# A hybrid decoder trunk: the last tile before each output projection signals its channel tiles as it reads them, and new high and low parts are written while it still runs

## The chip, the cores and the metric

The kernel runs on one core of a Trainium2 chip. The metric is the device time of one execution in microseconds (us), as the median of several runs.

## The reference, cut to what matters

One step of two layers for 512 prompt tokens and 64 sampled tokens (8 sequences of 8), 576 tokens in all, 2048 channels, in float32:

```python
# layer 0: attention (A) and gated DeltaNet (B) share one input projection
h = rms_norm(x, norm_gain[0])
qa, ka, va, za, qkv_b, a_b, b_b, z_b = split_even(h @ w_in_even[0])
o_a = attention(qa, ka, va) * silu(za)            # channels 0..1023 of the output's input
o_b = rms_norm(delta_rule(...)) * silu(z_b)       # channels 1024..2047
x = x + concatenate([o_a, o_b]) @ w_out_even[0]   # first output projection
# layer 1: Conformer convolution module
h = rms_norm(x, norm_gain[1])
val, gate, z = split(h @ w_in_odd[0], 3)
c = layer_norm(conv31(val * sigmoid(gate)) + conv_b)
y = silu(c) * silu(z)
x = x + y @ w_out_odd[0]                          # second output projection
out = rms_norm(x, final_norm_gain)                # and the new caches and states
```

## The kernel before

Activations lie channel-major: 16 channel tiles of 128 channels by 576 tokens, each kept three times. `full[:, k, :]` holds tile k in float32, `act_hi[:, k, :]` a rounded high part, `act_lo[:, k, :]` the rest (`full - act_hi`). Weights are split in the same way into `w_hi` and `w_lo`, in two slots. A product of one weight tile (128 output channels) is 96 matmuls of 128x288: for each of the 16 channel tiles and each half of the tokens `w_hi*act_hi`, `w_hi*act_lo` and `w_lo*act_hi`. They add up in one of two PSUM slots, `acc`. A **tile** below is such a set of 96 matmuls. All tiles stand in one list; `N_OUT0` and `N_OUT1` are the first tiles of the two output projections, `N_OUT0 - 1` (the last gate tile of the attention branch, `za`) and `N_OUT1 - 1` (the last `z` tile of the convolution module) are the tiles just ahead of them.

The order on each engine is written out by hand, and engines wait for one another on counting semaphores. TensorE runs tile after tile: `proj` (line 577) does a pair of channel tiles, e = 0 to 7, and counts `w_used` after e = 3 and e = 7; `first_tile` (line 604) does the first tile of an output projection in another order, high parts first and low parts `LOW_LAG` steps behind (12 in the first projection, 2 in the second), with a wait for each channel tile's part (`ahi_done`, `alo_even`, `alo_odd`). ScalarE copies weights to `w_hi` (`split_hi`) and channel tiles to `act_hi` (`act_split`; both are line 1088), computes the gate's tanh (`z_tanh`, line 1375, and `z_tanh_`, line 1481), and `affine` (lines 1487 and 1492). VectorE makes `w_lo` (`split_lo`) and every other tile of `act_lo` (`act_lo_even`; both line 1540), GpSimd the rest of `act_lo` (`act_lo_odd`, line 2268). SyncE issues the loads of weights (`w_raw`) and of the residual (`res`).

`act_hi` and `act_lo` exist once. The old parts are read by the last tile of the stage, so the new ones of the output projection are written after it:

```python
if turn == 1:
    act.wait_ge(w_used, 2 * n0)      # all of tile N_OUT0 - 1 has been read
    act_split(turn, 0, 8)            # channel tiles 8..15 (DeltaNet)
    act.wait_ge(gated, 1)            # sampled columns of tiles 0..7 are gated
act_split(turn, 8)                   # channel tiles 0..7 (attention)
```

In the first projection, `za_product(i)` on VectorE gates channel tile i of the attention branch with the product of gate tile i: it scales the prompt's columns of `full[:, i]`, and puts the gate of the sampled columns aside in `zs_samp`. Behind the last one, two instructions gate the sampled columns of tiles 0 to 7 together; the first of them lets SyncE load the residual (`res_free`), the second lets ScalarE go on (`gated`). Before them VectorE waits for stores of caches (`out_small`, `vnew_stored`).

In the second projection, step t of a loop on ScalarE and VectorE runs while TensorE does z tile t. `LN_Y` says at which t a channel tile's normalised value goes through `affine` and the two products that give y (`y_done`); tiles 13 and 14 stand at t = 15, tile 15 at t = 16, which is the time of tile `N_OUT1`, behind `act_split(3, 0, 6)`, the last `z_tanh_` and `act_split(3, 6, 8)`.

## Time and profile before

| what | value |
|---|---|
| median of 3 runs | 2012.45 us (2009.88 to 2012.73) |
| the profiled execution | 2012.49 us, of which the span is 2010.7 us |
| TensorE (PE) busy | 1966.4 us, 98% of the span |
| VectorE (DVE), ScalarE (ACT), GpSimd (POOL) busy | 1234.1, 733.6, 669.4 us |
| mean granted TensorE clock | 0.995 |

The span is the time from the first to the last instruction in the trace. In a timeline row the first number is the start in us from the beginning of the span, the second how long the row's instructions took together, `xN` how many there are, and the bracket how long the engine stood idle before and whose work ended that. PEld is the weight load of TensorE, SPq and ACTq the DMA issues of those engines.

### The profile page before, as it was taken

The numbers are of one execution on the slowest core, as the hardware profiler recorded it, in microseconds if no ns is written. First come the engines' busy times: TensorE is split into PE (matmuls) and PEld (weight loads), VectorE is DVE, ScalarE is ACT, GpSimd is POOL, SyncE is SP. The second block draws the span as 40 slices with busy tenths as digits, with TensorE's granted clock in tenths as the row PEclk, the third lists the DMA queues.
The fourth block names the chain that finished last, engine by engine and source line by source line (L and its number), as shares of the span: only waits on it lengthen the run. The fifth ranks groups of instructions, "written<-read, shape, count | busy, mean of one in ns | idle before, by whom it ended". The sixth has DMA issues, their size and how long they took to land.

```text
span 2010.7 us, 37345 instructions
## 1 busy us (share of the span) xinstructions
PE 1966.4 (98%) x15596; PEld 1905.2 (95%) x15596; DVE 1234.1 (61%) x2458; ACT 733.6 (36%) x1268; POOL 669.4 (33%) x659
## 2 busy tenths in 40 slices
PE   6999999999999999999999999999999999999997
PEld 4999999999999989898999999999999999999997
DVE  6566666656663436663433389999999954463334
ACT  5422222222222124552312255555555533342220
POOL 5123212321231121001211158888888850021110
PEclk9999999999999999999999999999999999999999
DMA  6211212212122334121444333333333222223333
GB/s 194 74 64 56 64 65 64 65 56 75 54 73 84 116 117 161 53 64 58 128 131 132 108 107 92 90 91 95 95 95 94 87 77 73 85 81 120 105 103 117
DMA packets 79721, 184.14 MB, mean 92 GB/s; under 512 B 26776, under 2 KB 35928, under 8 KB 79304
## 3 DMA queue, kind: packets, MB, share of 16 engines
q1 hardware_dynamic: 72304, 166.22, 27.0%
q0 software_dynamic: 3504, 9.63, 1.4%
q10 hardware_dynamic: 3744, 5.90, 0.8%
q8 instruction: 123, 2.02, 0.4%
q14 instruction: 46, 0.38, 0.1%
HBM read 162.66 MB, written 19.06 MB: 90 GB/s over the span
## 4 chain that ended last, share of the span: by engine, by line
PE 49%; DVE 2%; issue 0%; ACT 0%; DMA 0%; POOLq 0%; POOL 0%; DVEq 0%
PE acc L577 46%; PE acc L649 2%; DVE full L1543 1%; DVE act_lo L1540 1%; PE acc L604 1%; DVE w_lo L1540 0%; PE gp L619 0%; PE acc L677 0%; PE acc L666 0%; DMA w_raw<-wt 0%; PE gp L628 0%; ACT act_hi L1088 0%; DVE full L1540 0%; ACT w_hi L1088 0%; DVE arena L1581 0%
## 5 line engine op out<-in xcount | busy, mean ns | idle before, releaser
L577 PE MATMUL acc<-act_hi,w_hi 128*128 128x288 f32 x3904 | 860.8, 302 | 0.4 <-DVE w_lo L1540 0.3
L577 PE MATMUL acc<-act_hi,w_lo 128*128 128x288 f32 x3904 | 836.5, 296 | 0.0
L577 PE MATMUL acc<-act_lo,w_hi 128*128 128x288 f32 x3904 | 835.8, 296 | 0.0
L577 PEld LDWEIGHTS acc<-act_hi,w_hi 128*128 128x128 f32 x3904 | 624.9, 189 | 14.8 <-issue 9.5
L577 PEld LDWEIGHTS acc<-act_hi,w_lo 128*128 128x128 f32 x3904 | 628.8, 189 | 0.0
L577 PEld LDWEIGHTS acc<-act_lo,w_hi 128*128 128x128 f32 x3904 | 627.8, 189 | 0.0
L2268 POOL TENSOR_TENSOR arena<-arena 128x512 f32<-128x512 f32 (+2 forms) x281 | 387.0, 1377 | 347.6 <-ACT arena L1384 283.9
L1088 ACT ACTIVATE w_hi<-w_raw 128x1024 fp32r<-128x1024 f32 x264 | 277.1, 1054 | 420.6 <-PE acc L577 308.7
L1540 DVE TENSOR_TENSOR w_lo<-w_raw,w_hi 128x1024 fp32r<-128x1024 f32 x264 | 380.5, 1461 | 41.3 <-ACT w_hi L1088 40.5
L1543 DVE SCALAR_TENSOR_TENSOR gp<-arena,par,gp 128x64 f32<-128x64 f32 (+1 forms) x688 | 248.2, 445 | 0.0
L1088 ACT ACTIVATE arena<-arena,par 128x512 f32<-128x512 f32 x240 | 165.1, 720 | 96.4 <-POOL arena L2268 88.6
L1540 DVE TENSOR_TENSOR full<-acc,arena 128x576 f32<-128x576 f32 (+1 forms) x36 | 24.8, 689 | 232.9 <-PE acc L577 215.0
L2268 POOL TENSOR_TENSOR arena<-arena,cst 128x24 f32<-128x24 f32 (+2 forms) x82 | 31.3, 393 | 266.4 <-DVE arena L1543 109.8
L2268 POOL TENSOR_TENSOR act_lo<-full,act_hi 128x288 fp32r<-128x288 f32 (+1 forms) x48 | 57.7, 1223 | 157.8 <-ACT act_hi L1088 157.7
L2268 POOL TENSOR_TENSOR small<-small 128x4 f32<-128x4 f32 (+5 forms) x87 | 47.6, 552 | 141.2 <-DVE small L1547 76.2
L2268 POOL TENSOR_TENSOR full<-full,cst 128x512 f32<-128x512 f32 x40 | 60.5, 1521 | 66.3 <-PE gp L773 49.9
L1088 ACT ACTIVATE arena<-gp 128x512 f32<-128x512 f32 (+5 forms) x54 | 27.8, 540 | 133.7 <-PE gp L879 49.7
L1543 DVE SCALAR_TENSOR_TENSOR arena<-arena,small 128x512 f32<-128x512 f32 (+2 forms) x145 | 68.5, 515 | 0.3
L1543 DVE SCALAR_TENSOR_TENSOR arena<-arena,acc 128x576 f32<-128x576 f32 x24 | 18.0, 750 | 80.2 <-ACT arena L1481 74.0
L1088 ACT ACTIVATE act_hi<-full 128x288 fp32r<-128x288 f32 (+1 forms) x96 | 45.3, 516 | 33.4 <-DVE full L1543 29.1
L1088 ACT ACTIVATE full<-gp 128x256 f32<-128x256 f32 (+1 forms) x40 | 15.2, 379 | 113.7 <-PE gp L773 107.3
L1540 DVE TENSOR_TENSOR full<-full,gp 128x576 f32<-128x576 f32 (+2 forms) x72 | 32.8, 489 | 32.0 <-PE gp L788 26.2
(263 smaller groups left out, 1792.2 us busy)
## 6 DMA issues: line engine op xcount, KB each, us to landing
w_raw<-wt SPq DMA_DIRECT2D x264, 512.0 KB, 4.0
full<-x SPq DMA_DIRECT2D x16, 288.0 KB, 6.7
arena<-x SPq DMA_DIRECT2D x16, 288.0 KB, 3.6
arena<-x_scratch SPq DMA_DIRECT2D x16, 288.0 KB, 2.8
x_scratch<-full ACTq DMA_DIRECT2D x14, 288.0 KB, 4.0
out_y<-full SPq DMA_DIRECT2D x24, 144.0 KB, 1.9
arena<-state_in SPq DMA_DIRECT2D x6, 512.0 KB, 4.1
out_sdn<-arena POOLq DMA_DIRECT2D x6, 512.0 KB, 3.1
```

The lines of the kernel that those rows point to most:

```text
L577: ins = pe.matmul(acc[:, s, i, 0:HALF], w[:, s, wk], a[:, k, i * HALF:(i + 1) * HALF], start=(k == 0 and j == 0), stop=(k == KT - 1 and j ...
L604: ins = pe.matmul(acc[:, s, i, 0:HALF], w[:, s, wk], a[:, k, i * HALF:(i + 1) * HALF], start=(not low and pos == 0 and j == 0), stop=(low ...
L649: ins = pe.matmul(acc[:, s, a, 0:HALF], w[:, s, wk], x_[:, k, token_half(a)], start=(k == 0 and j == 0), stop=(k == KT - 1 and j == 2))
L1088: return act.activation(out, in_, ACT.Copy, scale=scale)
L1540: return dve.tensor_tensor(out, a, b, op)
L1543: return dve.scalar_tensor_tensor(out=out, in0=a, scalar=scalar, in1=b, op0=op0, op1=op1)
L2268: return pool.tensor_tensor(out, a, b, op)
```

## The change

For the last tile before each output projection, TensorE counts a new semaphore, `act_used`, after each pair of channel tiles that has no `w_used` of its own. `act_split` waits for the pair that it overwrites instead of for the whole tile.

In the first projection the order of the channel tiles becomes 0 to 5, 8 to 15, 6, 7. ScalarE begins twelve of them ahead of the last gate tanh, and the other four behind it. Sampled columns of tiles 0 to 6 are gated during tile `N_OUT0 - 1`, behind the gating of tile 6, and those of tile 7 by themselves behind the gating of tile 7. The waits for the stores move from VectorE to SyncE, in front of its loads of the residual.

In the second projection, channel tile 15 moves from t = 16 to t = 15, and its first product with it ahead of the last `z_gate`. `act_split(3, 0, 6)` goes to t = 15, six more follow ahead of the last `z_tanh_`, three behind it, and tile 15 comes last. `act_lo_even` goes along.

```diff
@@ -175,7 +175,7 @@
 
 LN_SQ = {3: range(0, 6), 4: range(6, 12), 5: range(12, 16)}
 LN_Y = {7: (0, 1), 8: (2, 3), 9: (4, 5), 10: (6, 7), 11: (8, 9)} | {k + 2: (k,) for k in range(10, 13)}
-LN_Y |= {15: (13, 14), 16: (15,)}
+LN_Y |= {15: (13, 14)}
 SAD = counts(["bias0", "bias1", "bias2", "max", "max2", "neg", "sub", "den", "inv", "prob", "turned_new",
               "out0", "out1"])
 SAA = counts(["exp", "turned", "v_new0", "v_new1"])
@@ -207,7 +207,7 @@
 def split_order(turn):
 
 
-    return [(k + 8) % KT for k in range(KT)] if turn == 1 else list(range(KT))
+    return [*range(6), *range(8, KT), 6, 7] if turn == 1 else list(range(KT))
 
 
 def blk(c):
@@ -359,6 +359,7 @@
         sdn_stored = [sem(f"sdn_stored{i}") for i in range(4)]
         ys_done = sem("ys_done")
         gated, halved = sem("gated"), sem("halved")
+        act_used, half_y = sem("act_used"), sem("last_y_without_gate")
         samp_pe, samp_dve = sem("samp_pe"), sem("samp_dve")
         samp_act, samp_pool = sem("samp_act"), sem("samp_pool")
 
@@ -370,7 +371,7 @@
         sa_pe, sa_dve, sa_act = sem("sa_pe"), sem("sa_dve"), sem("sa_act")
 
         res_in = [sem("res_in0"), sem("res_in1")]
-        res_free, x1_stored = sem("res_free"), sem("x1_stored")
+        x1_stored = sem("x1_stored")
 
         u_free, uprev_in = [sem("u_free0"), sem("u_free1")], [sem("uprev_in0"), sem("uprev_in1")]
         cf_stored = sem("cf_stored")
@@ -528,7 +529,9 @@
                 weights(n0)
                 weights(n0 + 1)
                 if n0 == N_OUT0:
-                    sp.wait_ge(res_free, 1)
+                    sp.wait_ge(gated, 1)
+                    sp.wait_ge(out_small, 16 * n_small)
+                    sp.wait_ge(vnew_stored, 32)
                 else:
                     sp.wait_ge(acc_free[0], N_VG // 2 + 1 + KT)
                     sp.wait_ge(x1_stored, 16 * X1_STORES)
@@ -563,7 +566,7 @@
 
         @block.tensor
         def _(pe):
-            def proj(m, s, e):
+            def proj(m, s, e, frees_act=False):
 
                 half = e // 4
                 if e % 4 == 0:
@@ -578,10 +581,12 @@
                                             start=(k == 0 and j == 0), stop=(k == KT - 1 and j == 2))
                 if e % 4 == 3:
                     ins.then_inc(w_used, 1)
-
-            def tile_of(m, s):
+                elif frees_act:
+                    ins.then_inc(act_used, 1)
+
+            def tile_of(m, s, frees_act=False):
                 for e in range(8):
-                    proj(m, s, e)
+                    proj(m, s, e, frees_act)
 
             def first_tile(n, turn):
 
@@ -1015,7 +1020,7 @@
                 n = N_Q + t
                 for e in range(8):
                     slot = 8 * t + e
-                    proj(n // 2, n % 2, e)
+                    proj(n // 2, n % 2, e, frees_act=(t == 15))
                     if slot == 0:
                         head_step(H - 1, 1, "o_chan")
                     if slot < ATT0 - 1:
@@ -1076,7 +1081,7 @@
             for i in range((N_Z1 + 7) // 2, N_OUT1 // 2):
                 tile_of(i, 0)
                 tile_of(i, 1)
-            tile_of(N_OUT1 // 2, 0)
+            tile_of(N_OUT1 // 2, 0, frees_act=True)
             out_section(N_OUT1, 3)
             half_sums(3, 1)
             spread_roots(NORM_END + 1, HALF_CHUNKS[1])
@@ -1106,8 +1111,15 @@
             def act_split(turn, first=0, last=KT):
 
                 for k in split_order(turn)[first:last]:
+                    e, half = k // 2, k // 8
                     if turn == 3:
                         act.wait_ge(y_done, k + 1)
+                    else:
+                        act.wait_ge(gated, 2 if k == 7 else 1)
+                    if e % 4 == 3:
+                        act.wait_ge(w_used, 2 * (N_OUT0 if turn == 1 else N_OUT1) - 1 + half)
+                    else:
+                        act.wait_ge(act_used, 6 * (turn // 2) + e + 1 - half)
                     copy(act_hi[:, k, :], full[:, k, :]).then_inc(ahi_done, 1)
 
 
@@ -1370,6 +1382,7 @@
                                     .then_inc(sa_act, 1)
 
             n = N_OUT0 - 1
+            act_split(1, 0, 12)
             tile_done(n // 2, n % 2)
             act.wait_ge(acc_free[1 - n % 2], (n - 1) // 2 + 1)
             act.activation(halves(za_t), acc_of(n % 2), ACT.Tanh, scale=0.5).then_inc(z_tanh, 1)
@@ -1386,11 +1399,7 @@
                         act.dma_start(x1_dram[j], full[:, j, :]).then_inc(x1_stored, 16)
 
 
-                if turn == 1:
-                    act.wait_ge(w_used, 2 * n0)
-                    act_split(turn, 0, 8)
-                    act.wait_ge(gated, 1)
-                act_split(turn, 8)
+                act_split(turn, 12 if turn == 1 else KT - 1)
                 split_hi((n0 + 1) // 2, (n0 + 1) % 2, 0)
                 split_hi((n0 + 1) // 2, (n0 + 1) % 2, 1)
                 for j in (1, 2):
@@ -1509,13 +1518,15 @@
                     if k >= 2:
                         act.wait_ge(c_summed, KT + k - 1)
                     act.activation(sqb[k % 2], full[:, k, :], ACT.Square).then_inc(ln_sq, 1)
-                if t == KT:
-                    act.wait_ge(w_used, 2 * N_OUT1)
+                if t == KT - 1:
                     act_split(3, 0, 6)
-                    z_tanh_(t - 1)
-                    act_split(3, 6, 8)
                 for k in LN_Y.get(t, ()):
                     affine(k)
+                if t == KT - 1:
+                    affine(KT - 1)
+            act_split(3, 6, 12)
+            z_tanh_(KT - 1)
+            act_split(3, 12, KT - 1)
             out_section(N_OUT1, 3)
             post_half(N_OUT1, 3, KT - 2, 1)
 
@@ -2020,6 +2031,13 @@
                                               gp[:, 2, 0:256].rearrange("p (j a c) -> p j a c", j=4, a=2)[:, :, a_, :])
                     ins.then_inc(sa_dve, 1)
 
+            def gate_samples(first, last):
+
+                for a_ in range(2):
+                    dst = full[:, first:last, a_ * HALF + HP:(a_ + 1) * HALF]
+                    ins = stt(dst, zs_samp[:, first:last, a_, :], 0.5, dst, MUL, MUL)
+                return ins
+
             own = lambda n_: dve.wait_ge(sa_dve, SAD[n_])
             for t in range(16):
                 n = N_Q + t
@@ -2039,19 +2057,18 @@
                         samp_att(SATT_DVE[slot - SATT0])
                     if e == 4 and t > 8:
                         za_product(t - 9)
+                        if t == 15:
+                            own("out1")
+                            for n_ in (N_ZA + 5, N_ZA + 6):
+                                dve.wait_ge(acc_free[n_ % 2], n_ // 2 + 1)
+                            gate_samples(0, 7).then_inc(gated, 1)
                     next_split(n // 2, n % 2, e)
-            act_lo_even(1, 8)
+
+            for k in split_order(1)[0:11:2]:
+                act_lo_even(1, k)
             za_product(7)
-
-            own("out1")
-            for n in (N_OUT0 - 2, N_OUT0 - 1):
-                dve.wait_ge(acc_free[n % 2], n // 2 + 1)
-            dve.wait_ge(out_small, 16 * n_small)
-            dve.wait_ge(vnew_stored, 32)
-            for a_ in range(2):
-                dst = full[:, 0:8, a_ * HALF + HP:(a_ + 1) * HALF]
-                stt(dst, zs_samp[:, :, a_, :], 0.5, dst, MUL, MUL).then_inc((res_free, gated)[a_], 1)
-
+            dve.wait_ge(acc_free[(N_ZA + 7) % 2], (N_ZA + 7) // 2 + 1)
+            gate_samples(7, 8).then_inc(gated, 1)
 
             def out_section(n0, turn):
                 def add_residual(m, s, j, jp, rnd):
@@ -2060,7 +2077,7 @@
                     dve.wait_ge(res_in[jp], 16 * rnd + (16 if turn == 1 else 16 + 8 * KT))
                     tt(halves(full[:, j, :]), acc_of(s), halves(res[jp]), ADD).then_inc(acc_free[s], 1)
 
-                for k in split_order(turn)[2 if turn == 1 else 8::2]:
+                for k in split_order(turn)[12 if turn == 1 else 10::2]:
                     act_lo_even(turn, k)
                 for half in range(2):
                     split_lo((n0 + 1) // 2, (n0 + 1) % 2, half)
@@ -2215,8 +2232,12 @@
             for t in range(1, KT + 1):
                 n = N_Z1 + t
                 if t == KT:
-                    for k in (0, 2, 4):
-                        act_lo_even(3, k)
+                    act_lo_even(3, 2)
+                    act_lo_even(3, 4)
+                    dve.wait_ge(ln_tanh, KT)
+                    stt(full[:, KT - 1, :], sqb[(KT - 1) % 2], 1.0, full[:, KT - 1, :], ADD, MUL).then_inc(half_y, 1)
+                    act_lo_even(3, 6)
+                    act_lo_even(3, 8)
                 if t > 1:
                     z_gate(t)
                 if 1 < t < KT:
@@ -2235,8 +2256,14 @@
                     dve.wait_ge(root_out, NORM_LN + 1)
                 for k in LN_Y.get(t, ()):
                     tt(halves(full[:, k, :]), halves(full[:, k, :]), rstd_ps, MUL).then_inc(ln_scaled, 1)
+                if t == KT - 1:
+                    tt(halves(full[:, KT - 1, :]), halves(full[:, KT - 1, :]), rstd_ps, MUL).then_inc(ln_scaled, 1)
+                    act_lo_even(3, 0)
                 if t == KT:
-                    act_lo_even(3, 6)
+                    k = KT - 1
+                    dve.wait_ge(half_y, 1)
+                    dve.wait_ge(acc_free[(N_Z1 + k) % 2], (N_Z1 + k) // 2 + 1)
+                    stt(full[:, k, :], full[:, k, :], 0.5, zring[k % ZRING], MUL, MUL).then_inc(y_done, 1)
                 for k in LN_Y.get(t, ()):
                     dve.wait_ge(ln_tanh, k + 1)
                     order(stt(full[:, k, :], sqb[k % 2], 1.0, full[:, k, :], ADD, MUL))
```

## Rows read from the trace of the kernel before

**Rows 1.** The page's first part: busy time, share of the span and instructions.
```profile
PE 1966.4 (98%) x15596; PEld 1905.2 (95%) x15596; DVE 1234.1 (61%) x2458; ACT 733.6 (36%) x1268; POOL 669.4 (33%) x659
```

**Rows 2.** Waits of PE over the span: us in total, times, longest.
```profile
PE acc L604 <- ACT act_hi L1088: 7.0, 4, 3.0
```

**Rows 3.** Stretches: length, busy us (count) of PE, PEld, DVE, ACT, POOL, granted clock, DMA share, GB/s.
```profile
933.40:946.30 12.90, 12.90 (x145) 12.58 (x144) 3.08 (x6) 0.00 (x0) 0.00 (x0) 1.00 0.26 81
946.30:965.80 19.50, 15.07 (x99) 14.64 (x98) 17.76 (x15) 11.83 (x19) 13.82 (x8) 0.91 0.10 31
965.80:978.60 12.80, 12.80 (x99) 12.80 (x98) 4.05 (x4) 3.75 (x4) 1.15 (x1) 1.00 0.65 211
...
1783.60:1802.58 18.98, 15.48 (x99) 14.45 (x97) 16.66 (x14) 13.28 (x21) 14.72 (x8) 0.91 0.00 1
```

**Rows 4.** Timeline of PE around the first projection's first tile.
```profile
946.03 0.42 PE L577 MATMUL acc<-act_hi,w_lo 128*128 128x288 f32 x2
947.86 0.50 PE L604 MATMUL acc<-act_hi,w_hi 128*128 128x288 f32 x2 [1.40 <-ACT act_hi L1088]
...
952.15 0.43 PE L604 MATMUL acc<-act_hi,w_lo 128*128 128x288 f32 x2
955.61 0.53 PE L604 MATMUL acc<-act_hi,w_hi 128*128 128x288 f32 x2 [3.03 <-ACT act_hi L1088]
...
956.95 0.68 PE L604 MATMUL acc<-act_hi,w_hi 128*128 128x288 f32 x2
...
959.83 0.54 PE L604 MATMUL acc<-act_lo,w_hi 128*128 128x288 f32 x2
...
965.80 0.43 PE L577 MATMUL acc<-act_hi,w_hi 128*128 128x288 f32 x2
```

**Rows 5.** Timelines of ACT and DVE there.
```profile
946.49 0.65 ACT L1375 ACTIVATE arena<-acc 128x576 f32<-128x576 f32 x1 [13.23 <-PE acc L577]
947.04 4.69 ACT L1088 ACTIVATE act_hi<-full 128x576 fp32r<-128x576 f32 x8
...
938.60 0.19 DVE L1987 COPY arena<-arena 128x64 f32<-128x64 f32 x1
938.70 1.22 DVE L1540 TENSOR_TENSOR w_lo<-w_raw,w_hi 128x1024 fp32r<-128x1024 f32 x1
...
951.88 2.96 DVE L1543 SCALAR_TENSOR_TENSOR full<-arena,full 128x256 f32<-128x256 f32 x2 [0.19 <-issue]
```

**Rows 6.** Timeline of PE around the second projection's first tile.
```profile
1783.34 0.43 PE L577 MATMUL acc<-act_hi,w_lo 128*128 128x288 f32 x2
1784.63 0.51 PE L604 MATMUL acc<-act_hi,w_hi 128*128 128x288 f32 x2 [0.86 <-ACT act_hi L1088]
...
1792.67 0.66 PE L604 MATMUL acc<-act_hi,w_hi 128*128 128x288 f32 x2 [1.69 <-ACT act_hi L1088]
...
1802.58 0.53 PE L577 MATMUL acc<-act_hi,w_hi 128*128 128x288 f32 x2 [0.35 <-DVE w_lo L1540]
```

**Rows 7.** Timelines of ACT, DVE and POOL there.
```profile
1772.03 0.63 ACT L1481 ACTIVATE arena<-acc 128x576 f32<-128x576 f32 x1
...
1775.64 1.41 DVE L1540 TENSOR_TENSOR full<-full,gp 128x576 f32<-128x576 f32 x2
1778.04 0.76 DVE L1543 SCALAR_TENSOR_TENSOR full<-arena,full 128x576 f32<-128x576 f32 x1 [0.99 <-ACT arena L1492]
...
1780.31 0.76 DVE L1543 SCALAR_TENSOR_TENSOR full<-full,arena 128x576 f32<-128x576 f32 x1
1784.52 0.76 DVE L1540 TENSOR_TENSOR act_lo<-full,act_hi 128x576 fp32r<-128x576 f32 x1 [3.45 <-ACT act_hi L1088]
...
1793.69 7.70 DVE L1540 TENSOR_TENSOR act_lo<-full,act_hi 128x576 fp32r<-128x576 f32 x4
1801.31 2.35 DVE L1540 TENSOR_TENSOR w_lo<-w_raw,w_hi 128x1024 fp32r<-128x1024 f32 x2
...
1793.27 7.50 POOL L2268 TENSOR_TENSOR act_lo<-full,act_hi 128x576 fp32r<-128x576 f32 x4 [0.91 <-ACT act_hi L1088]
```

## The prediction, made before the changed kernel was run

> **What bounds the kernel now.** I read the page's busy times first [rows 1]: TensorE is busy for 98% of the span, so a change can only win what TensorE still loses. Its list of waits comes next [rows 2]: of the waits that a software change can touch, the two `first_tile` runs (line 604) lose 7.0 us to high parts. A wait list misses slow matmuls, so I then measured both stretches from the last matmul pair of the old tile to the first of the next normal one [rows 3]. An undisturbed tile is 96 matmuls in 12.80 us, 0.133 us each, so a pair of them is due every 0.267 us. The two first tiles hold the same 96 matmuls but take 19.50 and 18.98 us: 6.70 and 6.18 us too much, 12.88 us together. That is the whole prize, 0.64% of the time.
>
> Where the 6.70 us lie in the first projection: the old tile's last pair starts at 946.03, the next would be due at 946.30 and starts at 947.86 (1.56 us) [rows 4], because ScalarE begins its high parts only at 947.04, after the tile's end and a tanh [rows 5]. After the first 8 channel tiles the pair due at 952.42 starts at 955.61 (3.19 us): the attention half waits for the gating of the sampled columns, two VectorE instructions at 951.88 that take 2.96 us. Then the matmuls run at 0.68 us a pair instead of 0.43, and the stretch has a granted clock of 0.91 where the next has 1.00: part of it ran at 1.2 GHz instead of 2.4. Six pairs from 956.95 to 959.83 take 2.88 us instead of 1.60, so 1.3 us. The remaining 0.65 us are a few more slow pairs, high parts that come every 0.57 us (8 take 4.69 us) while four matmuls eat one in 0.533 us, and small restarts. The second projection is alike [rows 6]: 1.03 us at the start (due 1783.60, starts 1784.63), 1.69 us of idling before 1792.67, about 1.7 us by a granted clock of 0.91 (0.09 x 18.98), and the other 1.8 us mostly late low parts and the next `w_lo`, for which PE waits at 1802.58.
>
> **The change, first projection.** The gating of tiles 0 to 6 now follows `za_product(6)`, whose last instruction ends at 938.79 [rows 5]. It is two instructions of 128x224. The nearest row, two of 128x256, took 2.96 us while GpSimd worked; GpSimd and ScalarE do nothing from 933.4 to 946.3 [rows 3], and the 128x64 copy there took 0.19 us. I take 0.4 us each, within 0.2 and 1.5: `gated` at 939.6 (939.2 to 941.8). The `w_lo` behind it moves by 0.8 us to 940.8; it is due at 946.3.
>
> ScalarE, idle before 946.49 for 13.23 us [rows 5], starts high parts at 939.7, one every 0.574 us: six by 943.2. Tiles 8 to 13 need `act_used` from e = 4, 5, 6. From the last e pairs back from 946.30 at 1.6 us each, e = 4, 5, 6 end at 941.5, 943.1, 944.7, so none of the six waits; the twelfth is done at 946.7. TensorE starts its first at 946.3 and needs one every 0.53 us, being seven to eleven ahead: the starting gap, the slow feed and the middle gap are gone, and with them the reason for the lower clock. The tanh moves from 946.49 to 946.7, behind the twelve.
>
> VectorE and GpSimd make the low parts from 940.8. Four pairs of them took 7.7 us where both worked [rows 7], 1.90 us a pair, though one alone on VectorE takes 0.76. So one blocks the other: 0.7 us for VectorE's, 1.2 for GpSimd's. Six on VectorE end at 940.8 + 0.7 + 5 x 1.9 = 951.0. Behind them stand, in VectorE's queue, `za_product(7)` (0.75, 0.7 and 0.2 us and up to 1.5 us of blocking: 954.2) and the gating of tile 7 (two of 128x32, taken at 0.2 us each because GpSimd has nothing left until tile 7's high part exists; up to 1.5 each): 954.6. Tile 7's high part is then ready at 955.3. TensorE wants it at its sixteenth step, 946.3 + 12 x 0.533 + 3 x 0.8 = 955.1. So about 0.2 us are lost, 2.8 at the upper bound. Then two low parts and the next `w_lo` follow: 958.4, due 959.1. First projection: 6.70 - 0.25 = **6.4 us won**.
>
> **Second projection.** ScalarE does six high parts in z tile 15 behind the tanh that ends at 1772.66 [rows 7]. It waits for e = 0, 1, 2 (1772.4, 1774.0 and 1775.6, counted back from 1783.60) and is done at 1777.0, before VectorE has scaled tile 13 for `affine`. VectorE's chain sets the end, so I follow it. Before, it finished y of tile 14 at 1781.07. Now GpSimd's first low part comes between the two `w_lo` (1.2 us), a third scaling by `rstd` is added (0.7), and the low part of tile 0 with its blocking (1.1); the 0.99 us of idleness ahead of 1778.04 absorbs as much. So 1781.07 + 1.2 + 0.7 + 1.1 - 1.0 = 1783.1. Then five instructions (low parts 2, 4, 6, 8 and the first product of tile 15) share with four of GpSimd's: 5 x 0.7 + 4 x 1.2 = 8.3, to 1791.4. `z_gate` and the last product of tile 15: 1.5, to 1792.9. Low parts 10, 12 and 14 and GpSimd's last: 3 x 0.7 + 1.2 = 3.3, to 1796.2. First `w_lo`: 1.2, to **1797.4**. TensorE alone would start the next tile at 1783.6 + 12.8 = 1796.4; low part 10 is 0.2 to 0.4 us late for it, the high part of tile 15 (1793.6) in time for 1795.1. Before, that tile started at 1802.58: **5.2 us won**; 6.2 if VectorE kept up, about 3.0 if each of its 11 instructions in that stretch took 0.2 us more.
>
> At this place the rows show 1.90 us for a low part on each of the two engines, against 0.76 us for one alone. The Trainium skill, SBUF — State Buffer, section Who interferes with whom, says that a VectorE instruction with two SBUF inputs and a GpSimd one that reads SBUF take a shared port exclusively, whoever comes first; that speaks against spreading low parts over a stage in which VectorE has work of its own. The trace agrees. Costed at 0.76 us each, VectorE would be done before TensorE and the second projection would win 6.2 us; by the rule, as by the row, 5.2.
>
> **What costs nothing.** The twelve new counts ride on matmuls. SyncE's new waits stand ahead of its residual loads and behind those all later weight loads; `gated` comes at 939.6, the stores' count was no wait on VectorE before (0.19 us idle before 951.88 [rows 5]), and the next weights cannot be asked for before a `w_lo` near 957. If a store were late the residual would still have until 959. Everything behind the first projection hangs on TensorE's progress and moves with it.
>
> **Sum.** 6.4 + 5.2 = 11.6 us. The profiled execution took 2012.49 us, 0.04 from the median: 2012.45 - 11.6 = **2000.9 us**.
>
> **The rivals.**
> (a) *A gap remains in one of the first tiles.* VectorE's queue with GpSimd's blocking is tight at 955.1 and 1793. If tile 7's gating is blocked (2.8 us) or low parts come 0.2 us later each (2.0 us), and a lower clock follows once more (1.3 to 1.7 us), some 4 us are lost: 2005. For it: the 2.96 us of the gating before. Against: GpSimd has no work at that moment. The Trainium skill, TensorE: Matmul & The Clock Gate, section HAM oscillation, says that idle gaps bring the slow clock back. The rows show it after the 3.19 us gap.
> (b) *One section gives nothing*, say since y of tile 15 now holds back the other tiles: 2012.45 - 6.4 = 2006.
> (c) *Given back later*, by a chain that does not start from TensorE: 2012. Against: no other engine is busy for more than 61% [rows 1].
> (d) *Slower.* All twelve high parts, and the tanh behind them in ScalarE's queue, now wait for one VectorE count. With `gated` at G the tile would end at about G + 0.7 + 12.8 + 0.4; that is 965.80 at G = 951.9, where the gating was before, and 4 us slower from 955.9 on: 2016 or more. It needs the gating 16 us later than reckoned, behind a `za_product(6)` that the trace shows done at 938.8.
> (e) *The change does not do what it says*: the signals would have to come late. They are counted for e other than 3 and 7, and `w_used` covers those, so this is within (b).
>
> **Chances.** Forecast 0.62 (its own range 1999 to 2003), (a) 0.20, (b) 0.09, (c) 0.05, (d) 0.04. A difference of 0.2%, 4 us, is about what a measurement can tell from none. Faster: 0.62 + 0.20 + 0.09 = 0.91; same 0.05; slower 0.04. The range goes from all 12.9 us won, less 1.3 us for the spread of the runs shown, 1998.3, to (b) at 2006.0.
>
> **What would show it.** In the changed trace, from the last pair of `N_OUT0 - 1` to the first of `N_OUT0 + 1`, some 13.0 us and a granted clock near 1.00; the same in the second, 13.7 us. The first high part near 939.7 and 1772.7; the gating two short rows near 939 and 954; no idle time of PE at line 604 above 0.5 us but for `w_lo` near the second's end. Wrong would be: another pause in the middle of either tile, a PE wait elsewhere that has grown by 5 us, or matmuls of 0.68 us a pair.

## The result, and the profile after

| | kernel before | changed kernel |
|---|---|---|
| time, median of the runs (us) | 2011.16 of 4 (2009.35 to 2012.73) | 1997.59 of 4 (1994.98 to 2001.81) |
| ratio, 95% interval | | 0.993 [0.9917, 0.9943] |
| profiled execution: time, span (us) | 2012.49, 2010.7 | 2001.81, 2000.0 |
| first tile of the first projection, due time to next tile (us) | 19.50 | 13.02 |
| first tile of the second projection (us) | 18.98 | 13.86 |

The "due time" of a first tile is when its first pair of matmuls would have started without a pause, 0.267 us behind the last pair of the old tile; its length runs from there to the first pair of the tile behind it.

The change makes the kernel faster, as forecast: by 0.7%, and the interval stays clear of 1. The forecast was 2000.9 us with a range from 1998.3 to 2006.0, and the measured median lies 0.7 us below that range. The two tiles that the change is about lost 6.48 + 5.12 = 11.6 us, which is the forecast sum to the tenth. So the miss is not in the steps of the change; the last group of experiments looks for where it is.

The page's first part, after [rows 1]: TensorE is busy for 3.8 us less, and the work of VectorE, ScalarE and GpSimd has changed by less than 1 us.

```profile
PE 1962.6 (98%) x15596; PEld 1902.4 (95%) x15596; DVE 1234.6 (62%) x2460; ACT 733.6 (37%) x1268; POOL 670.3 (34%) x659
```

The waits of PE, after (us in total, times, longest). The row of 7.0 us for high parts [rows 2] is gone. What is left of `first_tile`, now line 609, and of the tile behind it are two waits of 0.3 us, for a low part and for `w_lo`.

```profile
PE acc L609 <- DVE act_lo L1551: 0.3, 1, 0.3
PE acc L580 <- DVE w_lo L1551: 0.3, 1, 0.3
```

Stretches, after [rows 3]: first tile, the tile behind it, and the second projection's first tile. All three run at a granted clock of 1.00, and TensorE is busy for 13.02 of 13.02 us and 13.25 of 13.86.

```profile
946.52:959.54 13.02, 13.02 (x98) 12.82 (x97) 12.49 (x12) 5.19 (x8) 9.60 (x6) 1.00 0.02 3
959.54:972.34 12.80, 12.80 (x98) 12.80 (x97) 3.21 (x3) 3.75 (x4) 1.15 (x1) 1.00 0.69 208
1777.35:1791.21 13.86, 13.25 (x98) 12.76 (x97) 13.76 (x12) 7.20 (x12) 8.98 (x5) 1.00 0.01 1
```

Timeline of PE, first projection, after [rows 4]. The tile's first pair starts 0.26 us behind the old tile's last, as inside a tile; there is no pause at 952, and the pair of tile 7's high part is 0.13 us late (955.44, due 955.31).

```profile
946.25 0.42 PE L580 MATMUL acc<-act_hi,w_lo 128*128 128x288 f32 x2
946.51 0.43 PE L609 MATMUL acc<-act_hi,w_hi 128*128 128x288 f32 x2
...
955.04 0.43 PE L609 MATMUL acc<-act_lo,w_hi 128*128 128x288 f32 x2
955.44 0.53 PE L609 MATMUL acc<-act_hi,w_hi 128*128 128x288 f32 x2
...
959.54 0.42 PE L580 MATMUL acc<-act_hi,w_hi 128*128 128x288 f32 x2
```

Timelines of ACT, DVE and POOL there [rows 5]. The gating of tiles 0 to 6 is two instructions in 0.69 us at 939.13, with GpSimd idle. ScalarE starts high parts at 939.86 and has twelve by 946.87, when TensorE has only begun. VectorE's six low parts take 10.30 us because GpSimd works beside them, and `za_product(7)` is stretched too: its copy of 128x64 takes 1.41 us, where that of `za_product(6)`, with GpSimd idle, takes 0.19 [rows 5]. Tile 7's gating is short again (0.29 us for both), since GpSimd has run out of work, and its high part is ready at 955.39. The next `w_lo` is done at 959.52; GpSimd's last low part runs beside it.

```profile
939.86 7.01 ACT L1093 ACTIVATE act_hi<-full 128x576 fp32r<-128x576 f32 x12 [6.38 <-DVE full L1554]
...
954.70 0.69 ACT L1093 ACTIVATE act_hi<-full 128x576 fp32r<-128x576 f32 x1 [5.58 <-DVE full L1554]
...
939.13 0.69 DVE L1554 SCALAR_TENSOR_TENSOR full<-arena,full 128x224 f32<-128x224 f32 x2
...
940.88 10.30 DVE L1551 TENSOR_TENSOR act_lo<-full,act_hi 128x576 fp32r<-128x576 f32 x6
...
952.93 1.41 DVE L1998 COPY arena<-arena 128x64 f32<-128x64 f32 x1
954.38 0.29 DVE L1554 SCALAR_TENSOR_TENSOR full<-arena,full 128x32 f32<-128x32 f32 x2
...
956.37 3.15 DVE L1551 TENSOR_TENSOR w_lo<-w_raw,w_hi 128x1024 fp32r<-128x1024 f32 x2 [0.36 <-ACT w_hi L1093]
...
941.21 13.08 POOL L2295 TENSOR_TENSOR act_lo<-full,act_hi 128x576 fp32r<-128x576 f32 x7 [9.29 <-ACT act_hi L1093]
955.47 1.83 POOL L2295 TENSOR_TENSOR act_lo<-full,act_hi 128x576 fp32r<-128x576 f32 x1 [1.18 <-ACT act_hi L1093]
```

The second projection, DVE and PE, after [rows 6, 7]. Everything here is 6.25 us earlier than before, by what the first projection won. VectorE's chain is the one that the prediction followed: y of tile 14 done at 1776.95, four low parts and the first product of tile 15 until 1785.25 (the row shows the last two low parts), the last product of tile 15 until 1786.77, low parts until 1790.02, and then the first half of `w_lo`. TensorE waits for that half and starts the next tile at 1791.21.

```profile
1776.19 0.76 DVE L1554 SCALAR_TENSOR_TENSOR full<-full,arena 128x576 f32<-128x576 f32 x1
...
1781.37 3.88 DVE L1551 TENSOR_TENSOR act_lo<-full,act_hi 128x576 fp32r<-128x576 f32 x2
...
1786.01 0.76 DVE L1554 SCALAR_TENSOR_TENSOR full<-full,arena 128x576 f32<-128x576 f32 x1
1786.68 3.34 DVE L1551 TENSOR_TENSOR act_lo<-full,act_hi 128x576 fp32r<-128x576 f32 x3
1789.95 2.35 DVE L1551 TENSOR_TENSOR w_lo<-w_raw,w_hi 128x1024 fp32r<-128x1024 f32 x2
...
1791.21 0.53 PE L580 MATMUL acc<-act_hi,w_hi 128*128 128x288 f32 x2 [0.27 <-DVE w_lo L1551]
```

### The profile page after: what moved, and what is told of

The parts are those of the page before. It is cut to its first block, busy times and chain, and to the rows that moved or that the text cites. A ratio compares the mean times of both kernels' runs of the same rounds, so it can differ in the third digit from the quotient of the medians.

```text
span 2000.0 us, 37378 instructions
## 1 busy us (share of the span) xinstructions
PE 1962.6 (98%) x15596; PEld 1902.4 (95%) x15596; DVE 1234.6 (62%) x2460; ACT 733.6 (37%) x1268; POOL 670.3 (34%) x659
## 4 chain that ended last, share of the span: by engine, by line
PE 86%; DVE 10%; issue 1%; POOL 1%; ACT 1%; DMA 0%; SPq 0%; POOLq 0%; DVEq 0%; ACTq 0%
PE acc L580 71%; DVE arena L1551 2%; DVE full L1554 2%; PE acc L654 2%; DVE w_lo L1551 2%; PE gp L778 1%; DVE act_lo L1551 1%; PE acc L682 1%; POOL small L2295 1%; PE gp L788 1%; PE gp L884 1%; PE gp L770 1%; PE gp L936 1%; DVE full L1551 1%; PE gp L766 1%
```

## The experiments

The theory is that of the prediction: 11.6 us are won, 6.5 and 5.1 in the two tiles, and the lower median is chance in a measurement of four runs. The rival: the change wins some 13 us or more, the rest outside of the two tiles. In the runs below, "first tile" is measured as in the table above.

**Both kernels once more, and each projection alone.** The first two are the kernels as they are. The other two are the changed kernel with one projection put back as it was; in code, for the first of them:

```diff
-            tile_of(N_OUT1 // 2, 0, frees_act=True)
+            tile_of(N_OUT1 // 2, 0)
...
+                if t == KT:
+                    act.wait_ge(w_used, 2 * N_OUT1)
                     act_split(3, 0, 6)
+                    z_tanh_(t - 1)
+                    act_split(3, 6, 8)
```

and for the second:

```diff
-            act_split(1, 0, 12)
...
+                if turn == 1:
+                    act.wait_ge(w_used, 2 * n0)
+                    act_split(turn, 0, 8)
+                    act.wait_ge(gated, 1)
```

> The kernel before against itself. Both theories expect 0.0 us, within the interval that the comparison gives; its width and the spread of its runs say how much of a difference of 2 us can be chance. In its trace the two first tiles should again take 19.5 and 19.0 us; if their length varies from one execution to the next by 1 us or more, the price of these stalls was not a fixed number.

> The changed kernel again, with more runs. Theory 1 (the change wins what the two first tiles lost, and nothing else): 11.6 us faster, since the two stretches take 13.02 and 13.86 us in the trace instead of 19.50 and 18.98; the 13.6 us between the medians shown so far is then partly chance. Theory 2 (the stalls cost the kernel before more in most executions than in the profiled one, or the change wins something elsewhere as well): 13.6 us or more again.

> Only the first projection's part of the change; the second one's is as before. Theory 1: 6.5 us faster (19.50 - 13.02), the second first tile still 19.0 us. Theory 2: 7.5 us or more. Rival (c) of the prediction, given back later: clearly less than 6 us.

> Only the second projection's part. Theory 1: 5.1 us faster (18.98 - 13.86), the first first tile still 19.5 us, and with the run before it a sum of 11.6 us. Theory 2: 6 us or more. If the two parts help or hinder one another, the sum of the two differs from the whole.

| | time, median (us) | ratio to before | first tiles (us) |
|---|---|---|---|
| before | 2011.61 of 11 | 0.9996 [0.9987, 1.0005] | 19.37, 18.97 |
| changed | 1999.1 of 5 | 0.9937 [0.9925, 0.995] | 13.03, 13.87 |
| first projection alone | 2004.88 of 5 | 0.9963 [0.995, 0.9975] | 13.04, 18.96 |
| second projection alone | 2006.8 of 7 | 0.9977 [0.9967, 0.9988] | 19.37, 13.85 |

Each part shortens its own tile and leaves the other as it was. By the medians beside before (2012.08 of 17 in this group) they win 7.2 and 5.3 us, together 12.5, and the changed kernel wins 13.0. So both parts are needed and they add up. The 7.2 is 0.7 more than the tile shows, which these intervals, some 5 us wide, can't tell from nothing.

The kernel before gave one more reading. Its first tile ran at a granted clock of 1.00 this time, where the first profile had 0.91 [rows 3], and it still took 19.37 us. Here is the stretch (cut 0.17 us ahead of the due time, and 0.03 us longer), and then the waits of PE in the same execution, which count both first tiles:

```profile
943.80:963.20 19.40, 14.24 (x99) 13.22 (x97) 17.49 (x14) 11.84 (x19) 13.84 (x8) 1.00 0.10 31
```
```profile
PE acc L604 <- ACT act_hi L1088: 7.0, 4, 3.0
...
PE acc L604 <- DVE act_lo L1540: 1.1, 2, 0.6
...
PE acc L577 <- DVE w_lo L1540: 0.7, 2, 0.3
```

The pause for the gating is the same 3.0 us. With matmuls at full clock behind it, TensorE caught up with the low parts, and in this tile it waited 0.52 us for one of them and 0.34 us for `w_lo`. So VectorE let the next tile start 19.37 us after the due time and no sooner, and the lower clock, to which the prediction put down 1.3 us, cost 19.50 - 19.37 = 0.13 us. The kernel with the second projection alone shows the same 19.37 us, again at a granted clock of 1.00.

**All low parts on VectorE.** GpSimd's half of the low parts goes to VectorE, in both projections, and GpSimd does nothing there:

```diff
-                tt(act_lo[:, k, :], full[:, k, :], act_hi[:, k, :].bitcast(F32), SUB).then_inc(alo_even, 1)
+                tt(act_lo[:, k, :], full[:, k, :], act_hi[:, k, :].bitcast(F32), SUB).then_inc(alo_all, 1)
...
-            for k in split_order(1)[0:11:2]:
+            for k in split_order(1)[0:12]:
...
-                act_lo_odd(turn)
```

> The changed kernel with all 16 low parts of both first tiles made by VectorE; GpSimd makes none there. Theory 1 (while one of the two engines reads SBUF the other stands still, so a pair of low parts costs 0.7 + 1.2 us, and this sets the end of the second first tile): two on VectorE cost 1.4 us, it is done before TensorE needs it, both first tiles take 12.8 us (13.02 and 13.86 in the changed kernel), 1.3 us less in all, and no low part takes more than 0.8 us. Rival (the two engines help one another): 16 low parts on one engine take longer, and the first tiles grow by several us.

Both first tiles took 12.79 us, and the time was 1999.67 us (1999.17 to 2000.11), 0.9933 [0.992, 0.9945]. VectorE's timeline in the first projection:

```profile
938.57 8.11 DVE L1553 TENSOR_TENSOR act_lo<-full,act_hi 128x576 fp32r<-128x576 f32 x12
...
948.07 0.19 DVE L2000 COPY arena<-arena 128x64 f32<-128x64 f32 x1
948.29 0.29 DVE L1556 SCALAR_TENSOR_TENSOR full<-arena,full 128x32 f32<-128x32 f32 x2
948.50 2.76 DVE L1553 TENSOR_TENSOR act_lo<-full,act_hi 128x576 fp32r<-128x576 f32 x4
951.17 2.35 DVE L1553 TENSOR_TENSOR w_lo<-w_raw,w_hi 128x1024 fp32r<-128x1024 f32 x2
```

Twelve low parts take 8.11 us here, 0.68 us each, where the changed kernel's six took 10.30 us beside GpSimd, and the copy is back at 0.19 us. VectorE is done with `w_lo` at 953.52, 9.3 us after this tile's due time of 944.22, where the changed kernel took 13.0 (959.52, due 946.52). So one engine does the sixteen low parts sooner than two, and the last 1.3 us of the two tiles are gone. The Trainium skill, SBUF — State Buffer, section Who interferes with whom, says that a VectorE instruction with two SBUF inputs contends with a GpSimd instruction that reads SBUF; the trace agrees, with 1.72 us each for six low parts beside GpSimd and 0.68 us each for twelve without it.

**The signals and the new order, each without the other.** In the first kernel the new order stays and the signals aren't used: high parts wait until the old tile has ended.

```diff
-                    if e % 4 == 3:
-                        act.wait_ge(w_used, 2 * (N_OUT0 if turn == 1 else N_OUT1) - 1 + half)
-                    else:
-                        act.wait_ge(act_used, 6 * (turn // 2) + e + 1 - half)
+                    act.wait_ge(w_used, 2 * (N_OUT0 if turn == 1 else N_OUT1))
```

> The changed kernel, but every new high part waits until the whole last tile has been read, as in the kernel before; the order of tiles and the early gating stay. Theory 1 (VectorE's and ScalarE's queues set the end, and what stands behind a waiting instruction is late with it): the first projection's tile takes about 18 us, since the last gate tanh now waits behind twelve late high parts; the second's takes 22 to 23 us, since the affine of channel tiles 13 to 15 waits behind six; in all about 2 us slower than the kernel before. Rival (the signals close the gap at the start and nothing more): 1.6 and 1.0 us more than in the changed kernel, 14.6 and 14.9 us, still 9 us faster than before.

It took 2015.8 us (2012.19 to 2019.68), 1.0021 [1.001, 1.0031]: slower than before, by 3.5 us. The first tiles took 22.14 and 22.03 us. The second is as the theory had it; the first was expected at 18. ACT, then PE, in the first projection:

```profile
944.07 7.01 ACT L1093 ACTIVATE act_hi<-full 128x576 fp32r<-128x576 f32 x12 [13.29 <-PE acc L580]
...
958.56 0.68 ACT L1093 ACTIVATE act_hi<-full 128x576 fp32r<-128x576 f32 x1 [5.22 <-DVE full L1551]
```
```profile
959.29 0.85 PE L609 MATMUL acc<-act_hi,w_hi 128*128 128x288 f32 x2 [4.42 <-ACT act_hi L1093]
959.94 0.68 PE L609 MATMUL acc<-act_hi,w_lo 128*128 128x288 f32 x2
960.42 5.70 PE L609 MATMUL acc<-act_lo,w_hi 128*128 128x288 f32 x26
```

Against the tile's due time, 943.8 here and 946.5 in the changed kernel, the twelve high parts start 6.9 us later. So do VectorE's low parts, and `za_product(7)` and tile 7's gating stand behind these in its queue. TensorE waits 4.42 us for tile 7's high part and then does its matmuls at half clock. My expectation had left that queue out. This is the rival (d) of the prediction by another way: with 22.14 us against 19.50 before, the new order is worth having only with the signals.

In the second kernel the signals are used in the first projection, and the order of before stays: six high parts, those of tiles 8 to 13, are written while the old tile runs.

```diff
-            def proj(m, s, e):
+            def proj(m, s, e, frees_act=False):
...
+            for k in range(8, 14):
+                act.wait_ge(act_used, k // 2)
+                copy(act_hi[:, k, :], full[:, k, :]).then_inc(ahi_done, 1)
...
-                    act_split(turn, 0, 8)
+                    act_split(turn, 6, 8)
```

> The kernel before, second projection untouched; in the first only the signals are added: six DeltaNet high parts (tiles 8 to 13) are written while the last tile runs, the order of tiles and the place of the gating stay. Theory 1, followed along the queues: the tanh comes at the same time, but GpSimd has finished its low parts when the gating comes, so that ends near 951 instead of 954.9; the first tile takes about 15 us, 4.4 us won of the 6.5. Rival (the middle gap hangs on the gating, so what is won at the start is lost there): 19 us, nothing won.

It took 2008.6 us (2007.23 to 2013.34), 0.9983 [0.9974, 0.9993], with first tiles of 15.55 and 18.97 us, near the 15 of the theory. PE, then DVE and POOL, in the first projection:

```profile
949.54 0.53 PE L607 MATMUL acc<-act_hi,w_hi 128*128 128x288 f32 x2 [1.06 <-ACT act_hi L1091]
```
```profile
948.01 0.76 DVE L1549 SCALAR_TENSOR_TENSOR full<-arena,full 128x256 f32<-128x256 f32 x2 [0.19 <-issue]
...
946.12 1.65 POOL L2274 TENSOR_TENSOR act_lo<-full,act_hi 128x576 fp32r<-128x576 f32 x1 [0.69 <-ACT act_hi L1091]
```

The gating of 128x256 takes 0.76 us for two here and took 2.96 us before [rows 5]: GpSimd had done four low parts by 947.77 and stood idle. The pause in the middle shrinks from 3.0 to 1.06 us without any move of the gating. So of the 6.5 us six early high parts alone bring 3.9; the new order, with the early gating and twelve early high parts, brings the other 2.5.

**Where the executions differ.** The changed kernel was timed a third time together with the last three kernels, and had then 14 runs between 1994.98 and 2002.3 us. The two first tiles can't make that difference: they last 26.9 us in each profile, and 25.6 if each is an undisturbed tile of 12.80. So it was run three times more for its trace, and the kernel with all low parts on VectorE was timed once more beside it. In the table below, the span of each profiled execution is cut at four points: from its start to the due time of the first projection's first tile, that tile, the stretch to the second projection's first tile, that tile, and the tail behind it.

> The changed kernel once more, for its mean and for what varies between executions. Theory 1: 11.5 us faster over many runs; the two first tiles again 13.0 and 13.9 us, the rest of the span moving by up to 3 us with where the lower clock falls. Theory 2: 13 us or more again.

> The changed kernel once more, for its trace. Asked: where its executions, 1994.98 to 2002.3 us so far, differ. Theory: the two first tiles last 13.0 and 13.9 us in every execution, and the differences lie in stretches that the change does not touch: up to the first output projection (944.6 to 946.6 us so far), between the two first tiles (817.8 to 819.2 us), and the tail (208.8 us). An execution below 1998 us must then show one of these shorter by 2 us or more. Rival: the tight queue of VectorE makes the two first tiles differ by over 0.3 us from execution to execution; it can give at most 1.3 us in all, since 25.6 us is the least that both can last.

> As the run before it: first tiles of 13.0 and 13.9 us by the theory, and a time that follows from the other three stretches; first tiles that differ by over 0.3 us by the rival.

> As the two runs before it: first tiles of 13.0 and 13.9 us by the theory, and a time that follows from the other three stretches; first tiles that differ by over 0.3 us by the rival.

> All low parts of both projections on VectorE, timed once more beside the changed kernel. By the trace it is 0.2 + 1.1 us shorter in the two first tiles and 0.7 us in the tail: some 2 us below the changed kernel, and both first tiles 12.8 us again. Rival: the wins are given back in the stretch between the tiles, which took 820.5 us in its first trace against 817.8 to 819.2, and it is the same as the changed kernel, 1999 to 2000.5 us.

| changed kernel, profiled execution | time (us) | before first tile | first tile | between | first tile | tail |
|---|---|---|---|---|---|---|
| kernel before, for comparison | 2012.49 | 946.3 | 19.50 | 817.8 | 18.97 | 208.1 |
| first profile | 2001.81 | 946.5 | 13.02 | 817.8 | 13.86 | 208.8 |
| again (2nd) | 2001.88 | 946.6 | 13.03 | 817.8 | 13.87 | 208.8 |
| third | 2001.4 | 944.6 | 13.03 | 819.2 | 13.87 | 208.8 |
| fourth | 2002.06 | 946.8 | 13.00 | 817.8 | 13.86 | 208.8 |
| fifth | 2002.06 | 946.7 | 13.03 | 817.8 | 13.87 | 208.8 |
| sixth | 1997.02 | 946.1 | 13.00 | 817.6 | 13.88 | 204.7 |

The first tiles agree within 0.03 us in six executions, so the rival of these runs is out. The third timing gave 2001.4 us (0.9939 [0.9926, 0.9951]), the last three 0.9945, 0.9946 and 0.9933, with intervals of some 0.0036. In the third execution the stretch ahead of the first tile is 2 us shorter and the one between the tiles 1.4 us longer: its granted clock was low between 1640 and 1650 us (0.83 over these 10 us), where that of the fifth was low between 650 and 660 (0.83 too). Together these differences leave 0.7 us. The sixth execution is 5 us shorter, and 4.1 us of them lie in the tail, behind everything that the change touches. There is no wait in it that the others lack; the matmuls themselves come quicker. PE in the tail of the sixth execution, and then of the fifth:

```profile
1850.18 0.42 PE L580 MATMUL acc<-act_lo,w_hi 128*128 128x288 f32 x2
1850.44 0.42 PE L580 MATMUL acc<-act_hi,w_lo 128*128 128x288 f32 x2
1850.70 0.42 PE L580 MATMUL acc<-act_hi,w_hi 128*128 128x288 f32 x2
```
```profile
1850.19 0.43 PE L580 MATMUL acc<-act_lo,w_hi 128*128 128x288 f32 x2
1850.46 0.42 PE L580 MATMUL acc<-act_hi,w_lo 128*128 128x288 f32 x2
1850.73 0.43 PE L580 MATMUL acc<-act_hi,w_hi 128*128 128x288 f32 x2
```

A pair comes every 0.260 us in the one and every 0.267 in the other, both at a granted clock of 1.00. The sixth execution goes over to the quicker pace at the end of the second projection's first tile, at 1790.5, and keeps it until 1953; 2.5% of these 163 us are 4.1 us. The pace begins right behind the wait for `w_lo`, but the other five executions have that wait as well.

The fourth execution had the quicker pace too, from about 1183 to 1571 us. A stretch of it, the wait that came soon after, and PE around that wait:

```profile
1370.00:1470.00 100.00, 100.00 (x771) 100.00 (x770) 96.94 (x215) 57.15 (x78) 89.09 (x67) 1.00 0.33 88
...
1583.60:1591.46 7.86, 0.29 (x3) 0.07 (x2) 7.72 (x17) 3.59 (x6) 7.29 (x5) 0.84 0.38 133
```
```profile
1583.46 0.43 PE L580 MATMUL acc<-act_hi,w_lo 128*128 128x288 f32 x2
1591.46 0.82 PE L580 MATMUL acc<-act_hi,w_hi 128*128 128x288 f32 x2 [7.58 <-DVE arena L1554]
1592.08 0.68 PE L580 MATMUL acc<-act_lo,w_hi 128*128 128x288 f32 x2
```

There it brought nothing. TensorE was 9.4 us ahead at 1583 (the fifth execution does the same matmuls at 1593), met a VectorE that is busy for 97% of the time in that stage, waited 7.58 us for it and lost the other 1.9 us to matmuls at half clock behind the wait. The stretch between the first tiles is 817.8 us as in the others.

So the execution with the quicker pace in the tail was some 4 us shorter. Of the changed kernel's 20 runs eight lie between 1994.98 and 1999.1 us and twelve between 2000.83 and 2002.3; that the eight are those with the quicker tail was seen in one trace and is an inference for the other seven. Whether the kernel before has such executions is not shown: neither of its two traces has the quicker pace in the tail, and its 62 runs do not fall into two groups. In the first four runs three were of the eight; of the sixteen later ones five, and their median is 2001.41.

The kernel with all low parts on VectorE came to 1999.33 us (1997.86 to 2002.12), 0.9932 [0.9919, 0.9946], tiles 12.79 and 12.79 again. Over both times that it ran beside the changed kernel, its ten runs have a median of 1999.5 and the eleven of the changed kernel 2001.55, a difference of 2.0 us; by the means it is 1.2. In both of its traces the tiles are 1.3 us shorter. The shorter tail was there in the first (208.0 us) and not in the second (208.7). And as the rival had it, the stretch between the tiles took longer, 820.5 and 819.0 us: the clock was low in both between 1640 and 1660 us (0.73 and 0.92 over the two halves, then 0.88 and 0.95), where it was 1.00 in the fifth execution of the changed kernel. The second profiled execution took 2002.12 us, no less than those of the changed kernel. So the 1.3 us in the tiles are shown, and a gain in time is not: 2.0 us is half of what a measurement here can tell from none, and the rival is not excluded.

## Why the prediction was wrong, and where it was right

**The step that failed** is the lower end of the range: "all 12.9 us won, less 1.3 us for the spread of the runs shown". The 1.3 us is the term that was mis-sized. Three runs of the kernel before stood there; 62 of them lie between 2008.1 and 2016.39 us, and the changed kernel's 20 between 1994.98 and 2002.3. A median of four of these can lie over 3 us from that of all, 2001.1, and did. That three of the first four runs were quick ones is chance, as far as the runs show. The other half of the sentence took 12.80 us for a tile as TensorE's best. The quicker pace would make it 96 x 0.130 = 12.5, and in the tail of the sixth execution it was worth 4.1 us. That pace alone, 4.1 us below the forecast, would have put the lower end near 1997. What sets the pace stays open.

**The sum** was right. Forecast: 6.4 + 5.2 = 11.6 us; the tiles gave 6.48 + 5.12. Over all runs the medians are 2012.2 (62 runs) and 2001.1 (20), a difference of 11.1; the means, 2012.07 and 1999.96, differ by 12.1. Without the first four runs of each, which raised the question, the means are 2012.14 and 2000.45, a difference of 11.7, so 13 us or more is not borne out. The 13.6 us of the first measurement is a draw from these. The forecast ratio, 2000.9/2012.45 = 0.9943, lies in five of the six intervals of the changed kernel and at the upper end of the first. That the sum fits to the tenth is partly luck: the first tile's 6.48 us would be 6.35 by the other length of the old tile, 19.37 us, and the two profiled executions, before and after, differ by 10.7 us, since 0.7 of the 11.6 went in the tail and 0.2 ahead of the first tile.

**First projection**, forecast and measured (us): `gated` 939.6 and 939.82; first high part 939.7 and 939.86; twelfth 946.7 and 946.87; VectorE's sixth low part 951.0 and 951.18; `za_product(7)` 954.2 and 954.34; tile 7's high part 955.3 and 955.39; lost 0.25 and 0.22. Only `w_lo` was off: 958.4 and 959.52. VectorE waited 0.36 us for `w_hi` ahead of it, and GpSimd's last low part blocked it (3.15 us for two instead of 2.35), which the step had left out. It cost nothing: the next tile needs the first half at its start, at 959.54, and TensorE did not wait for it.

**Second projection**, forecast less the 6.25 us that all was earlier: 1776.85, 1785.15, 1786.65 and 1789.95 along VectorE's chain, and 1791.15 for the tile; measured 1776.95, 1785.25, 1786.77, 1790.02 and 1791.21. So 0.7 us for VectorE's low part and 1.2 us of blocking for GpSimd's was the right price, and the kernel with all low parts on VectorE shows that it was paid for nothing.

**The lower clock** was put down as a loss of its own in each tile, 1.3 and 1.7 us. The sum didn't rest on it, since it went from the tiles' whole lengths, but the reason was wrong. At full clock the first tile took 19.37 us, so the lower clock cost 0.13 us. In the second tile TensorE waited for `w_lo` at the end even with the lower clock [rows 6]: there too VectorE's late low parts and `w_lo` set the length, and the 1.7 us were no loss of their own.

**The rivals.** (a), (b), (d) and (e) didn't come: the gating wasn't blocked, both sections gave, `gated` came at 939.8, and no signal was late. Of (c) there is a small piece: in all six executions of the changed kernel TensorE's last six small matmuls (`spread_roots`) take 1.65 us at a lower clock instead of 0.94, and in the five without the quicker pace the tail is 0.7 us longer for it. In one trace each, the second projection's part alone has a tail of 208.8 us and the first projection's part alone 208.1, so it seems to come with the second part; but the kernel with all low parts on VectorE has it in one of two traces. Why the clock falls sooner there was not tried.

## What to carry to other kernels

Where a stage of TensorE is late at its start, measure it from the time when its first matmul was due to the time when the next undisturbed tile begins, and follow the queue of the engine that ends last instruction by instruction, with what one costs beside a busy GpSimd. That gave the 11.6 us that the two tiles lost. Early signals and a new order belong together: in the first projection's first tile the signals alone won 3.9 us, the order alone lost 2.6, and both won 6.5. And a range for a median needs the spread of single executions, of which three runs say little: look also for stretches in which the same instructions come at another pace.

## What the runs showed of the hardware that was not expected

- Matmuls of 128x288 come at two paces at the same granted clock of 1.00: a pair every 0.267 us or every 0.260. The quicker one held for 388 us in the fourth execution and for 163 in the sixth, and what sets it stays open.
- The same pause of 3.0 us of TensorE in the same kernel was followed by a granted clock of 0.91 over the tile in one execution and 1.00 in another. The lower clock of the first made the tile only 0.13 us longer, since VectorE's low parts and `w_lo` held the tile nearly as long. A pause of 1.06 us left it at 1.00; those of 4.42 and 7.58 us were followed by matmuls of 0.24 us instead of 0.133.
- VectorE alone was through the sixteen low parts and `w_lo` 3.7 us sooner (9.3 instead of 13.0 us after the tile's due time) than with GpSimd's help, and a copy of 128x64 beside a busy GpSimd took 1.41 us instead of 0.19.
